# Routing weights and coefficients of a retrieval layer moved by two key units at a time

## Chip, cores and metric

One core of one Trainium2 chip runs the whole program. The metric is device time in microseconds of that core. The kernel before takes 5941.4 us, the median of 3 runs (5940.6 to 5960.63). The profile shown here is of one further execution.

## The reference

One layer of a streaming encoder, for 512 prompt tokens and 8 streams of 16 tokens (640 tokens, five tiles of 128), width 2048, all in float32. A mixer (gated linear attention and a convolution branch) comes first. The part that matters here is the last one, a retrieval over 16,384 single-neuron experts:

```python
s1 = einsum(q[:, :, 0], k_sub1); s2 = einsum(q[:, :, 1], k_sub2)   # 8 heads, 128 keys each
v1, i1 = top_k(s1, 16); v2, i2 = top_k(s2, 16)
sc, pos = top_k(v1[:, None] + v2[None, :], 16)      # 16 of 256 pairs
idx = i1 * 128 + i2 (at pos); wts = softmax(sc)
act = gelu(u_exp[idx] . x)                          # 128 experts for a token
out = sum(wts * act * v_exp[idx])
x = x + gate * rms_norm(out)
```

## The kernel before

The mixer stages fill the first 3050 us and are not touched. Then come two functions.

`route` scores the keys, takes the top 16 and makes weights. For the first three tiles (384 tokens, `DN`) it spreads the weights into a dense table `d_w` in DRAM: for each of 128 key units (`NKEY`; a unit is 128 experts that share one second key) a plane of 128 partitions by 384 tokens, 192 KB. A half tile's weights gather in `w_buf`, and SP stores each half by one transfer of 4 MB in runs of 256 B (L1760), six in all. ACT waits for the store of the tile before, by `w_out`, when it comes to write the half again (L1869).

`experts` works on two groups of tokens at once.

- The first three tiles go densely, on TensorE. In the first phase, step n of 132 loads the two halves of unit n's `u_turned` (512 KB each) and one 512 KB half of `v_exp` for unit n-4, all into a ring of three buffers `x_stage`. ACT makes the high part of each (`x_hi`, L2170) and DVE the rest (`x_lo`, L2250), into rings of four. `score` multiplies them with the tokens (48 matmuls of 384 columns), ACT takes the GELU into `gob` (L2177), DVE multiplies by the weights in `gwr` (`weigh`, L2256), ACT stores the product into `d_gw` (`keep`, L2181) and splits it (`coef_high`, `coef_low`), and `add_up` multiplies it with the first 1024 columns of `v_exp` (18 matmuls of 512 columns). In the second phase, 128 units, the other 1024 columns of `v_exp` are loaded, with the coefficients read back from `d_gw` into `gwr`.
- The last two tiles go by gathers: POOL fetches rows of `u_exp` and `v_exp`, 1 MB a transfer, into `u_ring` and `v_ring`, four buffers each, and DVE does a dot product (L2268) or an accumulation (L2287) for each, laid between its other work in a fixed order (`gathered`).

Each engine runs its instructions in the written order. SP's order in the first phase is u, u, coefficients, v; in the second v, coefficients. A stage buffer is loaded again once `x_lo` of three items before is done (`lo_done`). `load_coefs` waits until the buffer's unit of four before has been used, and in the second phase for the store as well. `gwr` has four buffers of one unit and `gob` three, and each buffer has a semaphore for its transfers.

Of the kernel before, what the change touches and what calls it, by code (L numbers as in the profile page):

```python
# [13 lines left out]
F32 = mybir.dt.float32  # L14
F32R = mybir.dt.float32r
U32 = mybir.dt.uint32
ALU = mybir.AluOpType
ACT = mybir.ActivationFunctionType
AX = mybir.AxisListType

P = 128
# [21 lines left out]
NKEY = 128  # L43
# [24 lines left out]
ND = 3  # L68
DN = ND * P
# [59 lines left out]
def _build(nc, a, stack):  # L129
# [16 lines left out]
    def dram(name, shape, dt=F32):  # L146
        return nc.dram_tensor(name, shape, dt).ap()

    def sb(st, name, shape, dt=F32):
        return st.enter_context(nc.sbuf_tensor(name, shape, dt))  # L150
# [10 lines left out]
    d_x2, d_h2, d_q = (dram(n, (NTOK, D)) for n in ("d_x2", "d_h2", "d_q"))  # L161
    d_decay = dram("d_decay", (P, DK // P, 2 * TP + STREAMS))


    d_w = dram("d_w", (NKEY, P, DN))
    d_gw = dram("d_gw", (NKEY, P, DN))
    d_f3 = dram("d_f3", (P, D))
    d_post = d_mod[:, 5 * D:6 * D]


    kc = sb(stack, "kc", [P, K_END])
    area = -(-nc.sbuf_base // 32) * 32
    sb(stack, "act_area", [P, 2 * TT * KD * P])
    half = 4 * TT * KD * P
    act_hi = nc.alloc_sbuf_tensor_at("act_hi", [P, TT, KD, P], F32R, offset=area)
# [5 lines left out]
    ps = stack.enter_context(nc.psum_tensor("ps", [P, 8, NCOL], F32))  # L181
# [1519 lines left out]
    wt_all = sb(stack, "wt_all", [P, TT * SLOTS])  # L1701
    lk = link(None, "dve")
    route(nc, a, stage, sem, sb, kc, ps, (idx_all, wt_all), area, d_q, d_w, lk)
    experts(nc, a, stage, sem, sb, ps, (idx_all, wt_all), act_hi, act_lo, area, d_post, d_w, d_gw, d_f3, d_x2, d_h2)


def route(nc, a, stage, sem, sb, kc, ps, route_sb, area, d_q, d_w, lk):
# [12 lines left out]
    with stage() as (st, block):  # L1720
# [25 lines left out]
        @block.sync  # L1746
        def _(sp):
            sp.dma_start(keys[:], a["keys"]).then_inc(s_keys, 16)

            def queries(t):  # L1750
                if t > 0:
                    sp.wait_ge(q_turned, 4 * t)
                sp.dma_start(qt[:], d_q[t * P:(t + 1) * P, :].rearrange("p (j n) -> p j n", j=NH)).then_inc(s_q, 16)

            for t in range(ND):
                queries(t)
            for t in range(ND):
                for h in range(2):
                    sp.wait_ge(w_taken, t * NW + (h + 1) * NW // 2)
                    sp.dma_start(d_w[:, :, t * P + h * P // 2:t * P + (h + 1) * P // 2].rearrange("c p n -> p c n"),  # L1760
                                 w_buf[:, h]).then_inc(w_out[h], 16)
                if t + ND < TT:
                    queries(t + ND)
            for h in range(2):
                sp.wait_ge(w_out[h], 16 * ND)

        @block.gpsimd
        def _(pool):
# [59 lines left out]
        @block.scalar  # L1828
        def _(act):

            def turn(t):
                for g in range(4):
                    act.wait_ge(q_turned, t * 4 + (g + 1))
                    if g == 0 and t > 0:
                        act.wait_ge(sc_ready, 4 * t)
                    act.activation(q_t[:, 4 * g:4 * g + 4], ps[:, 4].rearrange("p (j n) -> p j n", j=4),
                                   ACT.Copy).then_inc(q_taken, 1)

            def scores(t):
                if t > 0:  # L1840
                    act.wait_ge(sc_free, t)
                for g in range(4):
                    act.wait_ge(sc_ready, t * 4 + (g + 1))
                    act.activation(sc[:, 4 * g:4 * g + 4], ps[:, g].rearrange("p (j n) -> p j n", j=4),
                                   ACT.Copy).then_inc(sc_copied, 1)

            def weights(t):
                act.wait_ge(s_ex, t + 1)
                act.activation(ex_t[:, 1], ex_t[:, 0], ACT.Exp).then_inc(s_exd, 1)

            def near(t, g):
                G = t * NW + g
                if G >= 2:
                    act.wait_ge(s_one1, G - 1)
                for j in range(4):
                    n = 4 * g + j
                    act.activation(dist[:, G % 2, j], iota, ACT.Abs, scale=-1.0,
                                   bias=id_t[:, t % 2, 0, n:n + 1]).then_inc(s_dist, 1)
                act.wait_ge(s_dist, 4 * G + 4)
                if G >= 2:  # L1860
                    act.wait_ge(w_ready, G - 1)
                act.activation(one1[:, G % 2], dist[:, G % 2], ACT.Relu, scale=-1.0, bias=1.0).then_inc(s_one1, 1)

            def take(t, g):
                G = t * NW + g
                act.wait_ge(w_ready, G + 1)
                h, n0 = 4 * g // (P // 2), 4 * g % (P // 2)
                if t > 0 and n0 == 0:
                    act.wait_ge(w_out[h], 16 * t)  # L1869
                act.activation(w_buf[:, h, :, n0:n0 + 4].rearrange("p c n -> p n c"),  # L1870
                               ps[:, 6 + G % 2].rearrange("p (n c) -> p n c", n=4), ACT.Copy).then_inc(w_taken, 1)

            turn(0)
            scores(0)
            turn(1)
            weights(0)
            for t in range(ND):
                act.wait_ge(id_ready, t + 1)
                act.activation(id_t[:, t % 2].rearrange("p a n -> p (a n)"), ps[:, 5, 0:3 * P], ACT.Copy).then_inc(id_taken, 1)
                act.wait_ge(id_taken, t + 1)  # L1880
                for g in range(NW):
                    near(t, g)
                    if g == 2:
                        scores(t + 1)
                    if g > 0:
                        take(t, g - 1)
                    if g == NW // 2:
                        turn(t + 2)
                take(t, NW - 1)
                weights(t + 1)  # L1890
            scores(TT - 1)
            weights(TT - 1)
# [75 lines left out]
                dve.sem_inc(route_done, 1)  # L1968


def experts(nc, a, stage, sem, sb, ps, route_sb, act_hi, act_lo, area, d_post, d_w, d_gw, d_f3, d_x2, d_h2):

    idx_all, wt_all = route_sb
    half = 4 * TT * KD * P
# [38 lines left out]
    with stage() as (st, block):  # L2013
# [2 lines left out]
        w_lo = sb(st, "x_lo", [P, DEPTH, UNIT], F32R)  # L2016
        u_ring = sb(st, "u_ring", [P, RING, D])
        v_ring = sb(st, "v_ring", [P, RING, D])
        gob = sb(st, "gob", [P, 3, DN])
        gwr = sb(st, "gwr", [P, 4, DN])  # L2020
        ss = sb(st, "x_ss", [P, TT, 4])
        st_in = [sem(f"x_in{n}") for n in range(3)]
        hi_done, lo_done, pe_used = sem("x_hidone"), sem("x_lodone"), sem("x_peused")
        gelu_done, gw_done = sem("x_gelu"), sem("x_gwdone")
        s_gw = [sem(f"x_gws{n}") for n in range(3)]
        gwr_in = [sem(f"x_gwr{n}") for n in range(4)]
        chi_done, clo_done, v_used = sem("x_chi"), sem("x_clo"), sem("x_vused")
        ev_done = sem("x_ev")
        h_in, f3_out, f3_in = [sem(f"x_h{g}") for g in range(NG)], sem("x_f3out"), sem("x_f3in")
# [12 lines left out]
        def _(sp):  # L2042
# [9 lines left out]
                load_item(v_item(m), a["v_exp"][c * P:(c + 1) * P, col:col + UNIT])  # L2052

            def load_coefs(j):
                if 4 <= j < NKEY + 4:
                    sp.wait_ge(gw_done, j - 3)
                elif j >= NKEY + 4:
                    sp.wait_ge(clo_done, j - 3)
                if j >= NKEY:
                    m = j - NKEY  # L2060
                    sp.wait_ge(s_gw[m % 3], 16 * (m // 3 + 1))
                sp.dma_start(gwr[:, j % 4], d_w[j] if j < NKEY else d_gw[j - NKEY]).then_inc(gwr_in[j % 4], 16)

            for n in range(STEPS):
                if n < NKEY:
# [98 lines left out]
        def _(act):  # L2164
# [6 lines left out]

            def gelu(n):
                act.wait_ge(pe_used, u_item(n, 1) + 1)
                if n >= 3:
                    act.wait_ge(clo_done, n - 2)
                    act.wait_ge(s_gw[n % 3], 16 * (n // 3))
                act.activation(gob[:, n % 3], ps[:, n % 2, 0:DN], ACT.Gelu).then_inc(gelu_done, 1)  # L2177

            def keep(n):
                act.wait_ge(gw_done, n + 1)  # L2180
                act.dma_start(d_gw[n], gob[:, n % 3]).then_inc(s_gw[n % 3], 16)  # L2181

            def coef_high(m):
                if m < NKEY:
                    act.wait_ge(gw_done, m + 1)
                    src = gob[:, m % 3]
                else:
                    act.wait_ge(gwr_in[m % 4], 16 * (m // 4 + 1))
                    src = gwr[:, m % 4]
                if m >= DEPTH:  # L2190
                    act.wait_ge(pe_used, v_item(m - DEPTH) + 1)
                act.activation(c_hi[:, m % DEPTH], src, ACT.Copy).then_inc(chi_done, 1)
# [53 lines left out]
        def _(dve):  # L2246
# [5 lines left out]

            def weigh(n):
                dve.wait_ge(gelu_done, n + 1)
                dve.wait_ge(gwr_in[n % 4], 16 * (n // 4 + 1))
                dve.tensor_tensor(gob[:, n % 3], gob[:, n % 3], gwr[:, n % 4], ALU.mult).then_inc(gw_done, 1)  # L2256

            def coef_low(m):
                dve.wait_ge(chi_done, m + 1)
                src = gob[:, m % 3] if m < NKEY else gwr[:, m % 4]  # L2260
                dve.tensor_tensor(c_lo[:, m % DEPTH], src, c_hi[:, m % DEPTH].bitcast(F32),  # L2261
                                  ALU.subtract).then_inc(clo_done, 1)

# [131 lines left out]
```

## Time and profile before

| | |
|---|---|
| median of 3 runs | 5941.4 us |
| the profiled execution's own time | 5952.3 us |
| its span | 5950.8 us |
| mean granted TensorE clock | 0.924 |
| `route` | about 3073 to 3562 us of the span |
| `experts`, first phase | 3568 to 5225 us |
| `experts`, second phase | 5231 to 5877 us |
| weights read, 192 KB each | 128 transfers |
| coefficients stored, 192 KB each | 128 transfers |
| coefficients read back, 192 KB each | 128 transfers |

Times in the views are microseconds from the span's start. PE is the matmul, PEld the weight load that lies beside it; a PE called busy need not be at its peak. The DMA share is the mean busy share of the core's 16 DMA engines.

### The profile page before, as it was taken

What the parts mean: (1) busy time and instruction counts of PE and PEld (TensorE: products, weight loads), DVE (VectorE), ACT (ScalarE), POOL (GpSimd) and SP (SyncE); (2) the same over time, 40 slices, a digit from 0 to 9 for tenths busy, and PEclk for the clock granted to TensorE, in tenths of its full rate; (3) what the DMA queues carried; (4) which work ended last, traced back from release to release, by engine and by line L of the source; (5) the groups of instructions that cost most, each with busy time, mean ns of one, the idle gap of its engine ahead of it and who ended that gap; (6) DMA issues with size and microseconds to landing.
All of it is one profiled execution on the core that took longest, in us unless ns stands there. A gap on an engine that the chain in (4) does not pass through costs nothing. (4 is left out here: it accounts for less than half of the span.)

```text
span 5950.8 us, 63220 instructions
## 1 busy us (share of the span) xinstructions
PE 5182.9 (87%) x23461; PEld 4191.4 (70%) x23461; DVE 3358.6 (56%) x4108; ACT 1857.6 (31%) x2516; POOL 1603.9 (27%) x1353
## 2 busy tenths in 40 slices
PE   8989999999987887996974639999999999978884
PEld 3347888888866335775754538999889889867773
DVE  7832211126753332222324456888778878878887
ACT  7743122222221111122316743333223323323332
POOL 0300000001001330000207952433333333344542
PEclk9989999999998998998985559999999999989997
DMA  9832332233323455333411329999999999999997
GB/s 355 309 120 91 113 104 84 93 105 113 108 84 127 169 174 187 129 112 127 124 54 36 92 59 379 376 383 374 366 367 383 369 384 380 372 378 411 405 409 309
DMA packets 467410, 1355.50 MB, mean 228 GB/s; under 512 B 137468, under 2 KB 194812, under 8 KB 383918
## 3 DMA queue, kind: packets, MB, share of 16 engines
q1 hardware_dynamic: 340500, 677.84, 32.2%
q0 software_dynamic: 99616, 633.82, 27.2%
q10 hardware_dynamic: 27072, 40.91, 2.0%
q8 instruction: 136, 2.23, 0.1%
q14 instruction: 86, 0.70, 0.0%
HBM read 1216.48 MB, written 137.04 MB: 227 GB/s over the span
## 5 line engine op out<-in xcount | busy, mean ns | idle before, releaser
L226 PE MATMUL ps<-w_hi,act_hi 128*128 128x512 f32 x3040 | 1193.5, 393 | 42.3 <-DVE act_lo L1031 23.0
L227 PE MATMUL ps<-w_lo,act_hi 128*128 128x512 f32 x3040 | 1188.3, 391 | 0.0
L228 PE MATMUL ps<-w_hi,act_lo 128*128 128x512 f32 x3040 | 1187.9, 391 | 0.0
L221 DVE TENSOR_TENSOR w_lo<-w_stage,w_hi 128x2048 fp32r<-128x2048 f32 x152 | 348.4, 2292 | 1258.7 <-ACT w_hi L217 1257.0
L2170 ACT ACTIVATE x_hi<-x_stage 128x1024 fp32r<-128x1024 f32 x512 | 543.4, 1061 | 1513.4 <-DMA x_stage<-u_turned 750.1
L2250 DVE TENSOR_TENSOR x_lo<-x_stage,x_hi 128x1024 fp32r<-128x1024 f32 x512 | 625.8, 1222 | 378.1 <-ACT x_hi L2170 374.5
L2097 POOL DMA_INDIRECT u_ring<-u_exp,idx_all x256 | 593.8, 2319 | 887.1 <-DVE u_ring L2268 812.0
L2124 PE MATMUL ps<-act_hi,x_hi 128*128 128x384 f32 x2048 | 694.0, 339 | 93.7 <-DVE x_lo L2250 90.6
L217 ACT ACTIVATE w_hi<-w_stage 128x2048 fp32r<-128x2048 f32 x152 | 291.1, 1916 | 1329.9 <-PE ps L228 1295.6
L2124 PE MATMUL ps<-x_hi,cx_hi 128*128 128x512 f32 x1536 | 614.6, 400 | 102.0 <-DVE cx_lo L2261 77.7
L226 PEld LDWEIGHTS ps<-w_hi,act_hi 128*128 128x128 f32 x3040 | 574.6, 189 | 166.0 <-issue 33.4
L2126 PE MATMUL ps<-act_hi,x_lo 128*128 128x384 f32 x2048 | 690.8, 337 | 0.0
L2125 PE MATMUL ps<-act_lo,x_hi 128*128 128x384 f32 x2048 | 690.7, 337 | 0.0
L227 PEld LDWEIGHTS ps<-w_lo,act_hi 128*128 128x128 f32 x3040 | 574.6, 189 | 120.7 <-issue 1.5
L228 PEld LDWEIGHTS ps<-w_hi,act_lo 128*128 128x128 f32 x3040 | 574.0, 189 | 120.0
L2126 PE MATMUL ps<-x_hi,cx_lo 128*128 128x512 f32 x1536 | 608.4, 396 | 0.0
L2125 PE MATMUL ps<-x_lo,cx_hi 128*128 128x512 f32 x1536 | 607.4, 395 | 0.0
L2287 DVE SCALAR_TENSOR_TENSOR acc<-v_ring,coef,acc 128x2048 f32<-128x2048 f32 x254 | 596.3, 2348 | 7.6 <-DMA v_ring<-v_exp,idx_all 6.3
L2268 DVE SCALAR_TENSOR_TENSOR u_ring<-u_ring,h_row 128x2048 f32<-128x2048 f32 x256 | 584.8, 2284 | 8.5 <-DMA h_row<-d_h 7.1
L2097 POOL DMA_INDIRECT v_ring<-v_exp,idx_all x256 | 350.4, 1369 | 555.8 <-DVE acc L2287 492.4
L2124 PEld LDWEIGHTS ps<-act_hi,x_hi 128*128 128x128 f32 x2048 | 386.5, 189 | 107.7 <-DVE x_lo L2250 102.6
L2124 PEld LDWEIGHTS ps<-x_hi,cx_hi 128*128 128x128 f32 x1536 | 292.2, 190 | 185.9 <-DVE x_lo L2250 102.2
(283 smaller groups left out, 6148.8 us busy)
## 6 DMA issues: line engine op xcount, KB each, us to landing
x_stage<-u_turned SPq DMA_DIRECT2D x256, 512.0 KB
x_stage<-v_exp SPq DMA_DIRECT2D x256, 512.0 KB
w_stage<-w_ada SPq DMA_DIRECT2D x96, 1024.0 KB, 6.4
w_stage<-w_in SPq DMA_DIRECT2D x96, 1024.0 KB, 5.1
d_w<-w_buf SPq DMA_DIRECT2D x6, 4096.0 KB, 20.9
gwr<-d_w SPq DMA_DIRECT2D x128, 192.0 KB
d_gw<-gob ACTq DMA_DIRECT2D x128, 192.0 KB
gwr<-d_gw SPq DMA_DIRECT2D x128, 192.0 KB
```

Source lines behind the costliest of these rows:

```text
L221: dve.tensor_tensor(w_lo[:, q % 2], w_in_st[:, q], w_hi[:, q % 2].bitcast(F32), ALU.subtract).then_inc(w_split, 1)
L226: pe.matmul(out, lhs[0], rhs[0], start=first, stop=False)
L227: pe.matmul(out, lhs[0], rhs[1], start=False, stop=False)
L228: return pe.matmul(out, lhs[1], rhs[0], start=False, stop=last)
L2097: pool.indirect_dma_start(out=ring[:, s % RING], out_offset=None, in_=a[table], in_offset=bass.IndirectOffsetOnAxis(ap=idx_all[:, col:col ...
L2124: pe.matmul(out, lhs[0], rhs[0], start=first, stop=False)
L2125: pe.matmul(out, lhs[0], rhs[1], start=False, stop=False)
L2126: return pe.matmul(out, lhs[1], rhs[0], start=False, stop=last)
L2170: act.activation(w_hi[:, i % DEPTH], stg[:, i % 3], ACT.Copy).then_inc(hi_done, 1)
L2250: dve.tensor_tensor(w_lo[:, i % DEPTH], stg[:, i % 3], w_hi[:, i % DEPTH].bitcast(F32), ALU.subtract).then_inc(lo_done, 1)
L2268: dve.scalar_tensor_tensor(out=u_ring[:, s % RING], in0=u_ring[:, s % RING], scalar=1.0, in1=h_row[:], op0=ALU.mult, op1=ALU.mult, accum_o ...
L2287: dve.scalar_tensor_tensor(out=acc[:], in0=v_ring[:, s % RING], scalar=coef[:, s:s + 1], in1=acc[:], op0=ALU.mult, op1=ALU.add).then_inc(a ...
```

## The change

The two tables have pairs of units as their first axis, and the two units of a pair lie beside each other in a partition's row: a pair's plane is 128 partitions by 3072 bytes, 384 KB. `gwr` becomes two buffers of a pair, and the first of them lies on the area of the constants `kc`, which the last stage doesn't read. `gob` has four units, seen as two pairs. `load_coefs` and `keep` do something for every second unit only. The stores of `w_buf` in `route` are two transfers of 2 MB each instead of one of 4 MB, with runs of 256 B as before.

```diff
-    d_w = dram("d_w", (NKEY, P, DN))
-    d_gw = dram("d_gw", (NKEY, P, DN))
+    d_w = dram("d_w", (NKEY // 2, P, 2, DN))
+    d_gw = dram("d_gw", (NKEY // 2, P, 2, DN))
...
-                    sp.dma_start(d_w[:, :, t * P + h * P // 2:t * P + (h + 1) * P // 2].rearrange("c p n -> p c n"),
-                                 w_buf[:, h]).then_inc(w_out[h], 16)
+                    at = slice(t * P + h * P // 2, t * P + (h + 1) * P // 2)
+                    for odd in range(2):
+                        sp.dma_start(d_w[:, :, odd, at].rearrange("c p n -> p c n"),
+                                     w_buf[:, h, odd::2]).then_inc(w_out[h], 16)
...
-                    act.wait_ge(w_out[h], 16 * t)
+                    act.wait_ge(w_out[h], 32 * t)
...
-        gob = sb(st, "gob", [P, 3, DN])
-        gwr = sb(st, "gwr", [P, 4, DN])
+        gob = sb(st, "gob", [P, 4, DN])
+        gwr = [at_sb("gwr0", [P, 2, DN], F32, offset=kc_at), sb(st, "gwr1", [P, 2, DN])]
...
             def load_coefs(j):
+                if j % 2 == 1:
+                    return
+                b = j // 2
                 if 4 <= j < NKEY + 4:
-                    sp.wait_ge(gw_done, j - 3)
+                    sp.wait_ge(gw_done, j - 2)
                 elif j >= NKEY + 4:
-                    sp.wait_ge(clo_done, j - 3)
+                    sp.wait_ge(clo_done, j - 2)
                 if j >= NKEY:
-                    m = j - NKEY
-                    sp.wait_ge(s_gw[m % 3], 16 * (m // 3 + 1))
-                sp.dma_start(gwr[:, j % 4], d_w[j] if j < NKEY else d_gw[j - NKEY]).then_inc(gwr_in[j % 4], 16)
+                    m = b - NKEY // 2
+                    sp.wait_ge(s_gw[m % 2], 16 * (m // 2 + 1))
+                sp.dma_start(gwr[b % 2][:], d_w[b] if j < NKEY else d_gw[b - NKEY // 2]).then_inc(gwr_in[b % 2], 16)
...
             def gelu(n):
                 act.wait_ge(pe_used, u_item(n, 1) + 1)
-                if n >= 3:
-                    act.wait_ge(clo_done, n - 2)
-                    act.wait_ge(s_gw[n % 3], 16 * (n // 3))
-                act.activation(gob[:, n % 3], ps[:, n % 2, 0:DN], ACT.Gelu).then_inc(gelu_done, 1)
+                if n >= 4:
+                    act.wait_ge(clo_done, n - 3)
+                    if n % 2 == 0:
+                        act.wait_ge(s_gw[n // 2 % 2], 16 * (n // 4))
+                act.activation(gob[:, n % 4], ps[:, n % 2, 0:DN], ACT.Gelu).then_inc(gelu_done, 1)
...
             def keep(n):
-                act.wait_ge(gw_done, n + 1)
-                act.dma_start(d_gw[n], gob[:, n % 3]).then_inc(s_gw[n % 3], 16)
+                if n % 2 == 1:
+                    act.wait_ge(gw_done, n + 1)
+                    act.dma_start(d_gw[n // 2], gob[:, n % 4 - 1:n % 4 + 1]).then_inc(s_gw[n // 2 % 2], 16)
```

`coef_high`, `weigh` and `coef_low` read the same units from the new places, and wait for the pair's transfer.

## Rows read from the trace of the kernel before

**Rows 1.** Busy time by engine in both phases and in the middle of the second.

```profile
core 0: us, PE busy (x) PEld busy (x) DVE busy (x) ACT busy (x) POOL busy (x), PEclk, DMA share, GB/s
3620.00:5200.00 1580.00, 1545.73 (x8078) 1440.52 (x8079) 1293.43 (x1137) 487.68 (x633) 596.76 (x335) 1.00 0.97 374
5260.00:5860.00 600.00, 528.96 (x2218) 419.86 (x2219) 516.34 (x465) 192.96 (x262) 280.74 (x140) 0.97 1.01 400
5400.00:5800.00 400.00, 357.74 (x1520) 283.46 (x1519) 356.96 (x321) 129.21 (x173) 200.46 (x98) 1.00 1.01 407
```

**Rows 2.** Waits in the first phase, 3620 to 5200: total, times, longest.

```profile
ACT x_hi L2170 <- DMA x_stage<-u_turned: 690.9, 219, 10.6
POOL u_ring L2097 <- DVE u_ring L2268: 487.4, 167, 9.2
PEld ps L2124 <- DVE x_lo L2250: 49.0, 41, 5.8
PE ps L2124 <- DVE x_lo L2250: 35.5, 34, 5.5
```

**Rows 3.** Waits in the second phase, 5260 to 5860, SP's own last.

```profile
ACT x_hi L2170 <- DMA x_stage<-v_exp: 301.6, 115, 19.0
ACT cx_hi L2192 <- DMA gwr<-d_gw: 79.8, 62, 1.9
DVE cx_lo L2261 <- ACT cx_hi L2192: 11.1, 16, 2.1
...
SPq L2062 <- DVE cx_lo L2261: 15.9, 12, 12.3
```

**Rows 4.** DMA queues in 5550 to 5800: packets, MB, share of 16 engines.

```profile
q0 software_dynamic: 8806, 64.15, 62.3%
q1 hardware_dynamic: 14885, 37.38, 38.7%
```

**Rows 5.** The same in 3900 to 4300.

```profile
q1 hardware_dynamic: 17719, 54.34, 36.9%
q10 hardware_dynamic: 4464, 6.10, 4.1%
```

**Rows 6.** The same in 60 to 160, and its loads (xcount, KB each, us to landing).

```profile
q1 hardware_dynamic: 4858, 35.34, 92.3%
...
w_stage<-w_ada SPq DMA_DIRECT2D x33, 1024.0 KB, 6.7
```

**Rows 7.** Order of time in the second phase: ACT, then SP's queue, then DVE.

```profile
5603.38 1.06 ACT L2170 ACTIVATE x_hi<-x_stage 128x1024 fp32r<-128x1024 f32 x1 [4.22 <-DMA x_stage<-v_exp]
5606.28 0.53 ACT L2192 ACTIVATE cx_hi<-gwr 128x384 fp32r<-128x384 f32 x1 [1.84 <-DMA gwr<-d_gw]
5607.42 1.06 ACT L2170 ACTIVATE x_hi<-x_stage 128x1024 fp32r<-128x1024 f32 x1 [0.61 <-DMA x_stage<-v_exp]
5608.83 0.53 ACT L2192 ACTIVATE cx_hi<-gwr 128x384 fp32r<-128x384 f32 x1 [0.35 <-DMA gwr<-d_gw]
...
5610.50 0.33 SPq L2048 DMA_DIRECT2D x_stage<-v_exp  x1
5610.93 0.38 SPq L2062 DMA_DIRECT2D gwr<-d_gw  x1
...
5609.26 1.22 DVE L2250 TENSOR_TENSOR x_lo<-x_stage,x_hi 128x1024 fp32r<-128x1024 f32 x1
5610.39 0.55 DVE L2261 TENSOR_TENSOR cx_lo<-gwr,cx_hi 128x384 fp32r<-128x384 f32 x1
```

**Rows 8.** SP's queue around the end of `route`, then the landing of `w_buf`'s stores.

```profile
3455.69 55.48 SPq L1760 DMA_DIRECT2D d_w<-w_buf  x2
3568.12 0.33 SPq L2043 DMA_DIRECT2D h_row<-d_h  x1
...
DMA to landing us min/median/max: 20.7/20.9/21.0
```

**Rows 9.** DMA issues of the whole span: count, KB each, median us to landing.

```profile
w_stage<-w_in SPq DMA_DIRECT2D x96, 1024.0 KB, 5.1
d_gates<-ob POOLq DMA_DIRECT2D x40, 256.0 KB, 2.3
```

More of the change, by code:

```diff
@@ L162, in _build @@
     d_decay = dram("d_decay", (P, DK // P, 2 * TP + STREAMS))
-    d_w = dram("d_w", (NKEY, P, DN))
-    d_gw = dram("d_gw", (NKEY, P, DN))
+    d_w = dram("d_w", (NKEY // 2, P, 2, DN))
+    d_gw = dram("d_gw", (NKEY // 2, P, 2, DN))
     d_f3 = dram("d_f3", (P, D))
     d_post = d_mod[:, 5 * D:6 * D]
+    kc_at = -(-nc.sbuf_base // 32) * 32
     kc = sb(stack, "kc", [P, K_END])
@@ L1703, in _build @@
     route(nc, a, stage, sem, sb, kc, ps, (idx_all, wt_all), area, d_q, d_w, lk)
-    experts(nc, a, stage, sem, sb, ps, (idx_all, wt_all), act_hi, act_lo, area, d_post, d_w, d_gw, d_f3, d_x2, d_h2)
+    experts(nc, a, stage, sem, sb, ps, (idx_all, wt_all), act_hi, act_lo, area, kc_at, d_post, d_w, d_gw, d_f3, d_x2, d_h2)
 def route(nc, a, stage, sem, sb, kc, ps, route_sb, area, d_q, d_w, lk):
@@ L1764, in _ @@
             for h in range(2):
-                sp.wait_ge(w_out[h], 16 * ND)
+                sp.wait_ge(w_out[h], 32 * ND)
         @block.gpsimd
@@ L1968, in _, with experts @@
                 dve.sem_inc(route_done, 1)
-def experts(nc, a, stage, sem, sb, ps, route_sb, act_hi, act_lo, area, d_post, d_w, d_gw, d_f3, d_x2, d_h2):
+def experts(nc, a, stage, sem, sb, ps, route_sb, act_hi, act_lo, area, kc_at, d_post, d_w, d_gw, d_f3, d_x2, d_h2):
     idx_all, wt_all = route_sb
@@ L2024, in experts @@
         gelu_done, gw_done = sem("x_gelu"), sem("x_gwdone")
-        s_gw = [sem(f"x_gws{n}") for n in range(3)]
-        gwr_in = [sem(f"x_gwr{n}") for n in range(4)]
+        s_gw = [sem(f"x_gws{n}") for n in range(2)]
+        gwr_in = [sem(f"x_gwr{n}") for n in range(2)]
         chi_done, clo_done, v_used = sem("x_chi"), sem("x_clo"), sem("x_vused")
@@ L2185, in coef_high @@
                     act.wait_ge(gw_done, m + 1)
-                    src = gob[:, m % 3]
+                    src = gob[:, m % 4]
                 else:
-                    act.wait_ge(gwr_in[m % 4], 16 * (m // 4 + 1))
-                    src = gwr[:, m % 4]
+                    act.wait_ge(gwr_in[m // 2 % 2], 16 * (m // 4 + 1))
+                    src = gwr[m // 2 % 2][:, m % 2]
                 if m >= DEPTH:
@@ L2254, in weigh @@
                 dve.wait_ge(gelu_done, n + 1)
-                dve.wait_ge(gwr_in[n % 4], 16 * (n // 4 + 1))
-                dve.tensor_tensor(gob[:, n % 3], gob[:, n % 3], gwr[:, n % 4], ALU.mult).then_inc(gw_done, 1)
+                dve.wait_ge(gwr_in[n // 2 % 2], 16 * (n // 4 + 1))
+                dve.tensor_tensor(gob[:, n % 4], gob[:, n % 4], gwr[n // 2 % 2][:, n % 2], ALU.mult).then_inc(gw_done, 1)
             def coef_low(m):
                 dve.wait_ge(chi_done, m + 1)
-                src = gob[:, m % 3] if m < NKEY else gwr[:, m % 4]
+                src = gob[:, m % 4] if m < NKEY else gwr[m // 2 % 2][:, m % 2]
                 dve.tensor_tensor(c_lo[:, m % DEPTH], src, c_hi[:, m % DEPTH].bitcast(F32),
```

## Prediction, made before the changed kernel ran

> **What bounds the kernel now.** I read the busy time of each engine by phase first [rows 1]. In the first phase (1580 us in the window) PE is busy 1546 us and the DMA engines have a share of 0.97: both are near their limit and no other engine is (DVE 1293). In the second phase the DMA share is 1.01, with DVE at 516 of 600 us and PE at 529: the DMA engines are the bound. Next come the waits. In the first phase ACT waits 691 us for `u_turned`, but of that only 35.5 us reach PE (49.0 us at its weight loads) [rows 2]. So all that faster transfers can give back there is 35 to 49 us. The gathers have slack: POOL waits 487 us for DVE to free a buffer. In the second phase ACT waits 302 us for `v_exp` and 79.8 us, 62 times, for a coefficient transfer, of which DVE feels 11.1 us [rows 3]. The change touches 75 MB of the traffic, not its size. It can act in four ways: fewer packets, fewer turns in a queue, other waits, other landings.
>
> **Packets.** Two queues in one window give the price of a packet. With share x 16 x 250 us as the time of all engines, q0 has 2492 us for 8806 packets and 64.15 MB, q1 1548 us for 14885 packets and 37.38 MB [rows 4]. Time = a x packets + b x MB solves to a = 9.8 ns and b = 37.5 us for a MB. Is a row of 3072 B one packet? A load of 1 MB whose partition row is likewise made of several blocks shows it: 33 loads and 4858 packets, 147 for each [rows 6], which is 128 rows of 8 KB and 16 closing packets, with a few of other loads. A pair thus takes 144 packets where two single transfers take 288. (31 stores in 400 us are just q10's 4464 packets, 144 each [rows 5].) Removed are 64 pairs x 3 kinds x 144 = 27,648 packets, x 9.8 ns / 16 engines = 16.9 us of DMA time: 11.3 us in the first phase (two kinds) and 5.6 us in the second.
> In the second phase, with the share at 1.01 [rows 1], I count 5 of the 5.6 us (the start, where PE catches up, isn't DMA-bound). In the first, DMA at 0.97 lies beside PE at 0.98, so I count half, 6 us. Bounds: 0 where PE covers it, 16.9 where nothing does. Sum -11.
>
> **Turns.** SP's queue carries weights and coefficients, and on the 16 engines it meets the gathers' packets of 8 KB. The coefficients behind one `v_exp` half land 2.90 us after that half (5603.38 to 5606.28) when gathers are under way, and 1.41 us after it, or less, when they are not [rows 7]. The bytes alone take 192 KB x 37.5 us/MB / 16 = 0.46 us, with 8 packets to an engine. The 2.4 us on top fit about eight gather packets of 8192 B x 37.5 us/MB + 9.8 ns = 0.317 us each: one of them ahead of each packet of the other queue. A pair has 8 packets on an engine where two units have 16, so SP's queue saves up to 8 x 0.317 = 2.5 us for each pair wherever gathers are pending. What it wins the gathers lose, and they have slack [rows 2]. The Trainium skill (DMA: Bandwidth & Descriptors, Queues, rings and completion order) says that an engine goes round robin between its queue rows at packet granularity; the two landings above agree with that, and what it would make of the time is the first rival.
> As a gain this is bounded by 0 (engines near saturation can only shift work) and by the rest of PE's 49 us. I take 5 us, near the low end, because the first phase is at 0.97 of the DMA already. Sum -5.
>
> **Waits and buffers.** First phase: SP comes to `load_coefs(j)` after loading u(j, 1), which waited for x_lo of u(j-1, 1). On DVE weigh(j-3), which the new wait wants, stands ahead of that x_lo in the same step. So the wait is met when SP arrives: 0. The pair lands two steps before its first use, as before: 0. gelu(n) now waits for coef_low(n-4) instead of (n-3), and for a store issued two steps before, on even units only: 0. `keep` issues 64 DMAs fewer on ACT and `load_coefs` 128 fewer on SP, both engines with hundreds of idle us: 0.
> Second phase: SP now waits for coef_low(j-3), which follows x_lo of the same unit on DVE. x_lo ends at 5610.48 and coef_low at 5610.94; SP's load of the next half runs from 5610.50 and its coefficients followed at 5610.93 [rows 7]. The new wait costs about 0.1 us on SP, with only the next `v_exp` load behind it, which waits for a later x_lo anyway. At the start SP already stands 12.3 us for coef_low [rows 3]; there it is one coef_low, 0.55 us, more. Together up to +1.
> Landing: the even unit of a pair now waits for 384 KB behind its `v_exp` half. In bytes that is 0.46 us more; the odd unit waits for nothing. ACT's 62 waits of 1.3 us on average become some 31 longer ones. DVE feels a late `cx_hi` in 16 of 124 units, 11.1 us [rows 3]. I take +1; bounds -11 (all of it gone) and +46 (third rival). Together +2.
> `route`: twelve stores instead of six, the same runs of 256 B. The last is issued at about 3511 and lands 20.9 us later, at 3532, while the next stage's first transfer comes at 3568 [rows 8]. A half of `w_buf` is written again only after the other, some 55 us on. DVE's routing of the last tiles hides it: 0. If that cover went, the last store would have to take over 57 us to be late. `gwr` on the constants' area: a barrier lies between: 0.
>
> **Sum.** -11 - 5 + 2 = -14 us. The profiled execution (5952.3 us, 1.5 of them around its span) would be 5938. It lies 11 us above the median of 5941.4, so the forecast for the median is 5927 us, which is -0.24%. Its own range is 5912 to 5946.
>
> **Rivals.**
> 1. *Turns decide: faster by over 0.5%.* The first phase's `x_lo` come in time and PE's gaps of 35 to 49 us nearly close, with the 5 us of the second phase: -45, 5896 us. For it: ACT waits for `u_turned` 219 times, and the gathers have time to give. Against it: the share of 0.97 leaves 47 us of 1580 idle on the DMA engines, and the gaps can't all close on that alone.
> 2. *Nothing measurable:* PE covers the first phase and DVE's order the second, or the rows go out in runs of 1536 B all the same (rows 6 speak against that): 5941 us.
> 3. *Slower: the pair is paid by its first unit.* Coefficients come in a burst, and `coef_low` of the even unit stands in DVE's queue ahead of two gathers' work and the next `x_lo`, which frees the stage buffer. If the second 192 KB costs another contended 2.90 us [rows 7] and half of the 64 even units meet it with DVE waiting, that is 32 x 2.9 = 93 us. DVE idles 84 of 600 us [rows 1] and can absorb about half: +46, 5987 us. It decides once DVE's wait for `cx_hi` is over some 60 us, from 11.1 now. Against it: only a quarter of ACT's waits reach DVE, and the odd unit's wait goes.
> 4. *Each transfer's fixed part counts.* From 256 KB in 2.3 us and 1024 KB in 5.1 us [rows 9], the part that doesn't grow with size is 1.4 us; 192 transfers fewer would be -263 us, 5678 us. Against it: the transfers lie beside others, and the engines are never empty. The Trainium skill (DMA: Bandwidth & Descriptors, Anatomy of one DMA) gives about 2.0 us a DMA, by which it would be -384 us; the DMA share of 1.01 says that this time is hidden.
>
> **Chances and range.** Forecast 0.55, first rival 0.17, second 0.15, third 0.11, fourth 0.02. 0.5% is 30 us, about what a measurement tells from no change here. Faster by more: 0.17 + 0.02 + 0.02 for the forecast's tail = 0.21. Slower by more: 0.11 + 0.01 = 0.12. Same: 0.67. The range 5893 to 5972 takes in the first rival and reaches 30 us above the median; the fourth rival, most of the third and the ends of the first are left out.
>
> **What the profile after would show.** Coefficient transfers x64 of 384 KB; about 27,600 packets fewer in all, with those under 2 KB gone down by some 49,000. The first phase's PE wait for `x_lo` at 25 to 45 us, the DMA share no higher. In the second phase ACT's waits for `gwr` at about half as many, each longer, and DVE's for `cx_hi` under 20 us. SP's first transfer of `experts` at 3568, give or take 2. Wrong would be: the same packet count (rival 2), DVE's wait for `cx_hi` at 60 us or more (rival 3), a first phase shorter by over 25 us (rival 1), or a change before 3562 us.

## The result: slower by 0.6%, not faster by 0.24%

| | before | changed |
|---|---|---|
| median | 5941.9 us (4 runs) | 5980.0 us (4 runs) |
| ratio, 95% interval | | 1.0062 [1.0038, 1.0086] |
| again, on the chip of the second batch | 5948.5 us | 5985.9 us, 1.0060 [1.0047, 1.0073] |
| the profiled execution's span | 5950.8 us | 5977.8 us |

Single executions of the kernel before lie between 5924 and 5968 us over all batches, so the comparisons below go by ratios within a batch. Two executions stood far out, one of e5 (9239.7 us) and one of e6 (6662.0 us), and are in no ratio.

Where the 27.0 us between the two spans lie, by the first SP transfer of each stage and the first eviction into `f_sum`: 6.2 us in the mixer, whose code is the same (it moves between 3070 and 3083 us over all the runs here), 2.8 in `route`, 17.1 in the first phase of `experts` and 0.9 after it. The rows of the changed kernel that show it: SP's queue, then the eviction.

```profile
3079.08 0.34 SPq L1749 DMA_DIRECT2D keys_sb<-keys  x1
...
3215.26 67.42 SPq L1763 DMA_DIRECT2D d_w<-w_buf  x4
3282.73 9.63 SPq L1754 DMA_DIRECT2D qt<-d_q  x1
...
3577.13 0.33 SPq L2046 DMA_DIRECT2D h_row<-d_h  x1
...
L2211 ACT ACTIVATE f_sum<-ps x6: 579/604/629, 5288.8 to 5291.2; 128x512 f32<-128x512 f32 x6
```

Before, the same points stood at 3072.9 (the load of the keys), 3568.1 [rows 8] and 5262.7 us:

```profile
L2203 ACT ACTIVATE f_sum<-ps x6: 577/602/632, 5262.7 to 5265.1; 128x512 f32<-128x512 f32 x6
```

The first phase as a whole, from SP's first `u_turned` load to the first eviction, before and then changed; after them the middle of the changed kernel's second phase, to be held against [rows 1] (the columns are those of [rows 1]):

```profile
3568.50:5262.70 1694.20, 1625.75 (x8448) 1512.42 (x8448) 1372.94 (x1204) 515.72 (x667) 647.34 (x366) 0.99 0.97 376
```

```profile
3577.51:5288.80 1711.29, 1634.23 (x8448) 1517.61 (x8448) 1370.38 (x1204) 512.69 (x667) 657.18 (x366) 0.98 0.95 373
5400.00:5800.00 400.00, 352.33 (x1498) 278.17 (x1498) 352.61 (x317) 126.99 (x173) 196.84 (x96) 1.00 1.00 402
```

In the first phase PE does the same 8448 matmuls. Half of the 17.1 us is PE standing, 77.1 us for 68.5, and half is the same matmuls keeping it busy 8.5 us longer, at a mean granted clock of 0.98 for 0.99 of full speed. The DMA share went down, to 0.95: the engines that I took for nearly full stand idle more often, in a stretch that takes longer. The waits in 3620 to 5200, first the one for `v_exp` before, then those of the changed kernel, against [rows 2]:

```profile
ACT x_hi L2170 <- DMA x_stage<-v_exp: 324.4, 114, 6.1
```

```profile
ACT x_hi L2176 <- DMA x_stage<-u_turned: 726.4, 227, 11.0
...
ACT x_hi L2176 <- DMA x_stage<-v_exp: 367.1, 93, 8.2
...
PE ps L2130 <- DVE x_lo L2258: 45.5, 37, 2.6
```

The waits for `v_exp` are fewer and longer: 93 of 3.9 us on average, where the kernel before had 114 of 2.8. In the second phase, against [rows 3], the waits for coefficients went from 62 to 43, and what DVE feels of them went down:

```profile
ACT cx_hi L2200 <- DMA gwr<-d_gw: 77.3, 43, 3.6
...
DVE cx_lo L2269 <- ACT cx_hi L2200: 8.9, 8, 2.1
```

The first phase's step, seen closely. In the changed kernel the pair's load (4611.60), the pair's store (4612.43) and a `v_exp` half (4612.83) are issued within 1.3 us, and ACT gets that half at 4627.63. Rows of SP's queue, then of ACT and its queue:

```profile
4611.60 0.43 SPq L2068 DMA_DIRECT2D gwr<-d_w  x1
4612.83 0.33 SPq L2051 DMA_DIRECT2D x_stage<-v_exp  x1
4618.44 4.21 SPq L2051 DMA_DIRECT2D x_stage<-u_turned  x2
...
4612.43 0.33 ACTq L2189 DMA_DIRECT2D d_gw<-gob  x1
...
4619.98 1.06 ACT L2176 ACTIVATE x_hi<-x_stage 128x1024 fp32r<-128x1024 f32 x1 [6.22 <-DMA x_stage<-u_turned]
4627.63 1.06 ACT L2176 ACTIVATE x_hi<-x_stage 128x1024 fp32r<-128x1024 f32 x1 [6.18 <-DMA x_stage<-v_exp]
```

One such stretch proves nothing. Over steps 10 to 125 I took the mean time from SP's issue of a `v_exp` half to the start of its `x_hi`: before 8.9 us in even steps and 10.9 in odd ones, changed 13.0 and 6.3. The mean over both is nearly the same (9.9 and 9.6); the even steps, in which both pair transfers fall, have it late.

### The profile page after: what moved, and what is told of

The parts are those of the page before. It is cut to its first block and busy times, and to the rows that moved or that the text cites. A ratio compares the mean times of both kernels' runs of the same rounds, so it can differ in the third digit from the quotient of the medians.

```text
span 5977.8 us, 62969 instructions
## 1 busy us (share of the span) xinstructions
PE 5195.8 (87%) x23461; PEld 4199.5 (70%) x23461; DVE 3355.6 (56%) x4108; ACT 1851.1 (31%) x2516; POOL 1617.7 (27%) x1353
## 2 busy tenths in 40 slices
DMA packets 439856, 1355.47 MB, mean 227 GB/s; under 512 B 134492, under 2 KB 142684, under 8 KB 356366
```

## Theories and experiments

*Meeting theory:* the load of one pair and the store of another fall into the same step, ahead of and beside `v_exp`. Its stage buffer comes free late, the next step has too little under way, and PE, at 98% of the phase, can't make up what it stood. *Burst theory:* every doubled transfer costs by itself. *Place theory:* the layout, the fourth unit of `gob` or the buffer on the constants' area costs. *Store theory:* the pair's store costs.

Edits are against the changed kernel unless said otherwise. "Phase" is the first phase in the profiled execution (1694.2 us before, 1711.3 changed). It is one execution each: the changed kernel's two differ by 5 us (1711.3 and 1716.6), and a profiled execution lay up to 13 us from the median of its kernel's executions. The ratios decide.

| run | loads | stores | ratio, interval | phase |
|---|---|---|---|---|
| e11 | single | single | 0.9997 [0.9986, 1.0008] | 1697.7 |
| e1 | single | pairs | 0.9995 [0.9983, 1.0006] | 1676.3 |
| e2 | pairs | single | 1.0007 [0.9992, 1.0021] | 1694.8 |
| e10 | two at once | single | 1.0028 [1.0016, 1.0041] | 1709.3 |
| e3 | two at once, old layout | single | 1.0038 [1.0023, 1.0053] | 1720.6 |
| e8 | pairs | pairs (the change) | 1.0060 [1.0047, 1.0073] | 1716.6 |
| e4 | pairs by halves | pairs | 1.0061 [1.0042, 1.0080] | 1721.9 |
| e5 | pairs, odd step | pairs | 0.9998 [0.9986, 1.0010] | 1680.7 |
| e6 | pairs | pairs, a step late | 0.9985 [0.9975, 0.9996] | 1677.1 |
| e7 | pairs, behind `v_exp` | pairs | 0.9993 [0.9981, 1.0004] | 1689.1 |
| e9 | pairs, behind `v_exp` | pairs, a step late | 0.9949 [0.9935, 0.9963] | 1653.2 |
| e14 | two at once, behind `v_exp` | pairs, a step late | 0.9989 [0.9978, 1.0000] | 1680.2 |
| e12 | single | single, a step late | 0.9989 [0.9978, 1.0000] | 1680.3 |
| e13 | single, behind `v_exp` | single, a step late | 1.0019 [1.0010, 1.0028] | 1698.1 |

### First batch: one half of the change at a time

**e1.** Each unit is loaded by itself:

```diff
...
-                if j % 2 == 1:
-                    return
...
-                sp.dma_start(gwr[b % 2][:], d_w[b] if j < NKEY else d_gw[b - NKEY // 2]).then_inc(gwr_in[b % 2], 16)
+                sp.dma_start(gwr[b % 2][:, j % 2], (d_w[b] if j < NKEY else d_gw[b - NKEY // 2])[:, j % 2]).then_inc(
+                    gwr_in[j % 4], 16)
```

> The changed kernel, but SP loads each unit's 192 KB by itself in every step (rows of 1536 B in the pair's plane, four semaphores); stores stay in pairs. Burst theory (a 384 KB load ahead of the v_exp load in every second step makes SP's queue lumpy, and the DMA engines run short in the other step): the first phase goes back from 1711 us to about 1694 to 1698, median about 5945 to 5955. Store theory (the pair's store, or what follows from it, costs): no change from the changed kernel, 5980. Place theory (the pair layout or the first pair buffer on the constants' area costs): 5980.

0.9995: the loss is gone, so neither the pair's store by itself nor the place costs.

**e2.** Each unit is stored by itself:

```diff
...
-                if n % 2 == 1:
-                    act.wait_ge(gw_done, n + 1)
-                    act.dma_start(d_gw[n // 2], gob[:, n % 4 - 1:n % 4 + 1]).then_inc(s_gw[n // 2 % 2], 16)
+                act.wait_ge(gw_done, n + 1)
+                act.dma_start(d_gw[n // 2][:, n % 2], gob[:, n % 4]).then_inc(s_gw[n % 4], 16)
```

> The changed kernel, but ACT stores each unit's 192 KB by itself in every step (four semaphores); loads stay in pairs. Burst theory of SP's loads: first phase stays near 1711 us, 5975 to 5985 us. Store theory: first phase near 1695 us, about 5950 us.

1.0007: gone as well. The burst theory had the loads alone at 5975 to 5985 us, and fell as it stood. Either half of the change is free; only both together cost.

**e3.** The kernel before, its two loads at once in the even step:

```diff
-            def load_coefs(j):
+            def load_coefs(j0):
+                if j0 % 2 == 1:
+                    return
...
+                for j in (j0, j0 + 1):
...
+                    sp.dma_start(gwr[:, j % 4], d_w[j] if j < NKEY else d_gw[j - NKEY]).then_inc(gwr_in[j % 4], 16)
```

> The kernel before with its layout, its buffers and its 192 KB transfers, but SP issues the two loads of a pair of units one behind the other in every second step; the new waits of the pair go with it. Burst theory: as slow as the changed kernel or slower, the first phase at 1705 to 1725 us, 5975 to 5990 us. Place theory, or large rows as the cause: no loss, 5942 us. My forecast's rule (turns between packets of two queues) has it slower than the changed kernel by up to 2.5 us for each contended pair in the first phase, 64 pairs.

1.0038. The burst costs here, and didn't in e2. Between the two lie the pair as one transfer with rows of 3072 B, and the layout with its buffers (e10 parts these two).

**e4.** In the first phase each step loads one half of the partitions of a pair:

```diff
...
+                    at = slice(j % 2 * P // 2, (j % 2 + 1) * P // 2)
+                    sp.dma_start(gwr[b % 2][at], d_w[b][at]).then_inc(gwr_in[2 * (b % 2) + j % 2], 16)
```

> The changed kernel, but in the first phase the pair's weights come as two transfers of 192 KB in two steps, 64 partitions each with rows of 3072 B; the second phase loads pairs. Burst theory: even work with large packets, the first phase back at 1690 to 1698 us and the median at 5935 to 5950 us. If large rows are the cause: first phase stays at 1711 us, 5980 us.

1.0061. The burst theory's 5935 to 5950 us missed, and the loss stayed, as I had expected if large rows were its cause. But the run changes more than I meant. Its queues over 3620 to 5200, those of the changed kernel first (packets, MB, share of 16 engines):

```profile
q0 software_dynamic: 47467, 345.70, 54.8%
q1 hardware_dynamic: 60997, 214.14, 35.9%
```

```profile
q0 software_dynamic: 47291, 344.32, 55.9%
q1 hardware_dynamic: 61597, 212.86, 37.7%
```

SP's queue took 0.377 x 16 x 1580 us / 212.86 MB = 44.8 us for a MB, for 42.4, and the gathers 41.0 for 40.1. With transfers of 64 partitions for a ninth of its bytes, SP's queue took 6% more DMA time for each MB. So this run doesn't tell whether an even load with large rows would have removed the loss. That large rows alone cause it is refuted below: e5 and e6 keep them without the loss. Why e4 is as slow as the change is open.

### Second batch: pull load and store apart

**e5.** The pair's weights one step later, in the odd step (`if j % 2 == (1 if j >= NKEY else 0): return`, then `j -= 1` in the first phase).

> The changed kernel, but in the first phase SP loads a pair's weights one step later, in the odd step; ACT stores the pairs in the steps that it did (its even ones). Coincidence theory (a pair's load and a pair's store fall into the same step, and together they delay v_exp there and leave the next step short of work): the loss goes, first phase 1680 to 1700 us, ratio to the kernel before 0.998 to 1.002. Plain burst theory (each burst costs by itself, the store's is added): no change, first phase 1705 to 1720 us, ratio 1.005. Against both: the weights land later before their use, which would show as DVE waiting for gwr.

**e6.** The store one step later:

```diff
-                if 3 <= n < NKEY + 3:
-                    keep(n - 3)
+                if 4 <= n < NKEY + 4:
+                    keep(n - 4)
```

> The changed kernel, but ACT issues a pair's store one step later, so that it falls into the step without a load. Coincidence theory: the loss goes, first phase 1680 to 1700 us, ratio 0.998 to 1.002. Plain burst theory: ratio 1.005. If the GELU then waits for the store of its buffer, ACT shows a wait for d_gw and the loss may stay for that reason.

**e7.** `load_v(n - LAGV)` stands ahead of `load_coefs(n)`.

> The changed kernel, but in the first phase SP issues v_exp ahead of the pair's load instead of behind it. If the loss comes by the late v_exp half (issue to landing 13 us in the step with the load, against 9 to 11 before), it goes or turns into a gain: ratio 0.996 to 1.002. If it comes by the next step being short of work, it stays: 1.004 to 1.007. The new wait's price may show as well: SP stands for x_lo of the v_exp item before it can issue the pair's load; the weights have two steps.

**e8.** The changed kernel again.

> The changed kernel once more, as the yardstick of this chip for the three others and for how far single executions spread: ratio 1.004 to 1.008, first phase 1700 to 1720 us.

0.9998, 0.9985 and 0.9993 beside 1.0060 for the change. e5 and e6 keep every transfer, its size and its layout, and move one of the two to the odd step, e5 the load and e6 the store: the meeting theory had both at 0.998 to 1.002, the burst theory at 1.005. e7 leaves both in the even step and only puts `v_exp` ahead of the load, and the loss is gone too: it also takes a `v_exp` behind the load. Means from issue to `x_hi` of the `v_exp` halves, even and odd: e8 13.2 and 6.1, e6 11.3 and 8.2, e7 9.3 and 9.9. e6's first phase, window and PE's waits:

```profile
3620.00:5200.00 1580.00, 1558.87 (x8146) 1457.09 (x8145) 1303.23 (x1143) 492.00 (x639) 602.37 (x337) 1.00 0.97 378
...
PE ps L2130 <- DVE x_lo L2258: 21.1, 22, 5.2
```

PE's wait for `x_lo` is 21.1 us, for 45.5 in the changed kernel, and the DMA share is back at 0.97. Over the whole first phase PE stands 51.4 us in e6 and 56.8 in e5, for 77.1 and 85.0 in the two profiled executions of the change.

### Third batch and after: both remedies, row size, layout

**e9.** e6 and e7 together.

> The changed kernel with both remedies: v_exp issued ahead of the pair's load in the first phase, and the pair's store one step later. If they take away the same loss (the meeting of load, store and v_exp), no more is gained than by the late store alone: ratio 0.997 to 1.000. If they act apart: 0.995 to 0.997.

**e10.** e2, its pair load as two transfers of 192 KB:

```diff
...
+                for one in range(2):
+                    sp.dma_start(gwr[b % 2][:, one], (d_w[b] if j < NKEY else d_gw[b - NKEY // 2])[:, one]).then_inc(
+                        gwr_in[2 * (b % 2) + one], 16)
```

> The changed kernel with stores of one unit in every step, and each pair's load as two transfers of 192 KB one behind the other in the even step: the run with single stores, but rows of 1536 B in the loads. If the row size is what made that run (1.0007) better than the bursts in the old layout (1.0038), this one is at 1.003 to 1.005, first phase 1705 to 1720 us. If the new layout or the fourth unit of gob did it, it stays at 1.000 to 1.0015.

**e11.** The edits of e1 and e2 together: layout and buffers alone.

> Only the layout and the buffers of the change: all loads and stores one unit in every step, rows of 1536 B, four units of gob, the first pair buffer on the constants' area, twelve stores in the routing stage. Every theory but the place theory has it as the kernel before: ratio 0.999 to 1.001. Place theory: 1.003 or more.

**e12.** e11 with e6's late store.

> As the run of layout and buffers alone, but each unit's store one step later. If the late store helps by itself, whatever the pairs (the store moves out of the way of something within the step), ratio 0.998 to 0.999 like the pairs with the late store (0.9985). If it helps only because pairs met: no change from the layout run, 1.000.

**e13.** e12 with e7's order.

> Layout and buffers of the change, loads and stores one unit in every step (rows of 1536 B), v_exp issued ahead of the weights and the store one step later. If the order alone gains: 0.994 to 0.996, as with pairs (0.9949). If pairs with large rows have a part in it: 0.996 to 0.999.

**e14.** e9 with e10's two loads.

> Pairs with both remedies, but each pair's load as two transfers of 192 KB one behind the other, rows of 1536 B; stores in pairs as they were. Row size decides in this order too (it was worth 0.0021 in the order of the change: 1.0028 against 1.0007): 0.996 to 0.998. If it matters only where the load stands ahead of v_exp: 0.9945 to 0.9955.

e9 at 0.9949 says that the two remedies act apart, not on one loss. e11 clears the place: 0.9997. e10 against e2 is the pair's load as two transfers with rows of 1536 B or as one with rows of 3072 B, issued at the same place: 1.0028 to 1.0007, about 12 us, 14.5 in the profiled first phase. Row size and number of transfers go together in this edit; no run parts them. e14 against e9 is the same edit in the better order: 0.9989 to 0.9949, 24 us, 27.0 in the phase. The late store takes 0.0075 off the pairs (e8 to e6) and 0.0008 off the single units (e11 to e12, whose intervals overlap): it is worth something measurable only where pairs meet. With `v_exp` first and no pairs the kernel is slower (e13, 1.0019), beyond what either theory expected, so e9's gain is not the order's alone: it takes pairs, loaded by one transfer with large rows, in the right order. Why the order costs the single units (e13 against e12) is open.

**The version that beats both** is e9, 0.9949 of the kernel before, 5927.4 us in its batch beside 5954.4. Its first phase:

```profile
3576.47:5229.70 1653.23, 1610.89 (x8448) 1509.01 (x8448) 1372.57 (x1204) 515.23 (x668) 640.20 (x366) 0.99 0.97 386
```

386 GB/s for 376 before and 373 in the changed kernel, at the share of before: the DMA engines move more in the same busy time.

## Why the prediction was wrong, step by step

- **What bounds the kernel.** Right that the first phase has little slack, wrong about what its DMA share of 0.97 means. I read it as nearly full whatever the order. It went to 0.95 in the changed kernel with a longer phase. And "all that faster transfers can give back there is 35 to 49 us" counted PE's waits alone. e9's profiled phase is 41 us shorter (the whole run 30 us, by its ratio), of which PE stands 26 us less and is busy 15 us less with the same matmuls, a part that the bound didn't hold. That 41 lies between 35 and 49 is luck.
- **Packets.** The count was right: 27,554 packets fewer (467,410 to 439,856), forecast 27,648, and those under 2 KB down by 52,128 (49,152 of them the rows forecast). 8655 packets and 62.99 MB in 61.8%, 11265 and 37.59 in 38.2% of the second phase's window give 8.7 ns a packet by the same sum as before (9.8). The 11 us that I counted for them didn't show: e2 has 18,338 packets fewer than the kernel before, at 1.0007.
- **Turns.** A gain of this sign exists, and its size is uncertain. A pair's load as one transfer instead of two is worth 14.5 to 27 us of the profiled first phase, for the loads only; packets' own time there is a third of 16.9, 5.6 us. The remaining 9 to 21 us are what I took as 5 for loads and stores. By the ratios of the whole run it is less: 12 and 24 us, of which the packets of both phases' loads are 11, so 1 and 13 us are left. That they come from turns between queues fits the sign and the bound of 2.5 us for each pair (0.1 to 0.3 for each of the 64 in the phase), but no run showed the turns themselves. Nor did the two landings: their 2.4 us are eight gather packets in all, and one ahead of each row or eight ahead of the whole transfer fit them alike.
- **Waits and buffers: the step that failed.** "`keep` issues 64 DMAs fewer on ACT ...: 0" and "the pair lands two steps before its first use, as before: 0". Each wait of an instruction was priced rightly; no new wait appeared. What I never priced is what 384 KB of load and 384 KB of store do to the other transfers of the step that they share. Moving either by a step removes the loss, 37 to 45 us for a whole run by the ratios of e5 and e6 against e8. Without the meeting the pairs measure -1 us (e5, interval -8 to +6) and -9 us (e6, -15 to -2), where I had -14.
- **The second phase** is +0.9 us in this pair of profiles, where I had -5 and +2: its DMA share was 1.00 and its rate 402 GB/s for 407. From the first eviction to the end, the eight profiled executions that load pairs there as one transfer take 687.1 us on average (682.0 to 693.5), the eight others 687.2 (685.4 to 689.3). So the 5.6 us of packet time didn't come out as time. Why is open.
- **`route`.** Forecast 0, measured +2.8 in this pair of profiles. With the 6.2 us of the mixer, SP's first transfer of `experts` came at 3577, where I had 3568. From the load of the keys to that transfer the two runs with the old layout take 494.8 and 495.2 us, twelve of the fourteen with the new one 497.2 to 498.9 and the other two 494.8 and 495.7: the layout's stores go with it. They hold SP's queue longer (67.42 us for 58.48 in the kernel before, for a tile's stores) and `qt` of the next tile goes out 9.2 us later after the load of the keys. That this delay is the cause was not tried.
- **Rivals.** The third had the right sign and nearly the size (+46, for +38 measured), but the wrong place, so that its size is luck: DVE's wait for `cx_hi` fell from 11.1 to 8.9 us, where 60 were wanted. The time came from the first phase, by a mechanism that I did not list. The first rival's gain exists in part (e9, 30 of its 45 us) but needs the order of issue changed with it, and turns as its cause weren't shown. The second's small rows are refuted by the packet count; its other half, fewer packets and nothing measurable, is what e1, e2 and e5 show once the meeting is gone. The fourth is refuted by e1 and e2, which took away 64 and 128 transfers, 88 and 175 us at its 1.4 us each, and gained nothing measurable.

What stays open: how the meeting does its harm within the step. The means from issue to `x_hi` rank the change worst, but e2 has 12.4 and 7.2 us with no loss, so they are a sign and not a measure.

## What to carry to other kernels

Before two transfers are merged, write down step by step what else is on the DMA queues then: two doubled transfers in one step cost 0.6% here, the same two a step apart nothing measurable or gained 0.15%, and a step apart with the stream that the others wait for issued ahead of the load the merge gained 0.5%. A DMA share of 0.97 was no proof that the order of issue is free, and waits that are all met don't show what a transfer does to its neighbours. Test a merged load and a merged store apart before judging either.

## What was not expected of the hardware

- One load of 384 KB with rows of 3072 B, instead of two of 192 KB with rows of 1536 B issued one behind the other, gave 0.2% (e2 against e10) and 0.4% (e9 against e14) of the kernel, the latter more than twice the packets' own price: 18,432 packets at 8.7 to 9.8 ns over 16 engines are 10 to 11 us, for 24.
- With a ninth of the bytes of SP's queue in transfers of 64 partitions (e4), a MB took 6% more DMA time on that queue (44.8 us for 42.4), and 2% more on the gathers' queue beside it (41.0 for 40.1).
